# Recurrent scan: 64x64 blocks turned by a transposition instead of by a product with the unit matrix, where the result lies in partitions 0 to 63

## The reference

```python
def rwkv7_step(S, inp):
    r, w, k, v, kk, kka = inp
    sa = jnp.einsum('dbhij,dbhj->dbhi', S, -kk)
    S = S * w[..., None, :] + sa[..., :, None] * kka[..., None, :] + v[..., :, None] * k[..., None, :]
    y = jnp.einsum('dbhij,dbhj->dbhi', S, r)
    return S, y
...
    S0 = jnp.zeros((N_DIR, B, RWKV_HEADS, HEAD_DIM, HEAD_DIM), jnp.float32)
    _, ys = lax.scan(rwkv7_step, S0, xs)
```

## Time and profile before

| | |
|---|---|
| median of three runs | 3591.16 us (3590.39 to 3597.05) |
| profiled execution, its own time | 3590.71 us |
| its span in the profile | 3588.8 us |
| TensorE matmul busy | 3439.0 us, 96% |
| TensorE weight load busy | 2840.0 us, 79% |
| VectorE busy | 1939.6 us, 54% |
| ScalarE busy | 1275.6 us, 36% |
| mean granted TensorE clock | 0.987 of full |

### The profile page before, as it was taken

How to read it: one execution, slowest core, us unless ns; L and a number is a source line. 1 busy time by engine, 2 the same in 40 slices (tenths; PEclk the granted TensorE clock), 3 DMA queues, 4 the chain that set the end, 5 groups by cost and what they waited for, 6 DMA issues and landing times.

```text
span 3588.8 us, 54631 instructions
## 1 busy us (share of the span) xinstructions
PE 3439.0 (96%) x22725; PEld 2840.0 (79%) x22725; DVE 1939.6 (54%) x2632; ACT 1275.6 (36%) x1637; POOL 13.9 (0%) x20
## 2 busy tenths in 40 slices
PE   9999999999999999999999989999899897999998
PEld 7778888887788877778887768888887885888887
DVE  4566646436574654575344455344677666755434
ACT  3474424324442332453223343222532113643223
POOL 0000000000000000000000000000000000000000
PEclk9999999999999999999999999999999999999999
DMA  4102322221122222113222212222224001122222
GB/s 157 59 1 94 103 96 94 94 94 48 65 90 104 94 92 95 51 59 105 94 94 99 88 51 92 103 94 94 93 104 144 16 5 40 58 82 99 99 95 71
DMA packets 50429, 297.06 MB, mean 83 GB/s; under 512 B 6847, under 2 KB 7871, under 8 KB 17348
## 3 DMA queue, kind: packets, MB, share of 16 engines
q1 hardware_dynamic: 39376, 269.92, 21.9%
q10 hardware_dynamic: 10868, 24.41, 1.9%
HBM read 283.99 MB, written 10.33 MB: 82 GB/s over the span
## 4 chain that ended last, share of the span: by engine, by line
PE 85%; DVE 9%; ACT 4%; issue 2%; ACTq 0%; DVEq 0%
PE PS L353 14%; PE PS L355 14%; PE PS L354 14%; PE PS L478 7%; PE PS L479 7%; PE PS L480 7%; PE PS L1997 2%; PE PS L1998 2%; PE PS L1999 2%; PE PS L2522 1%; PE PS L2525 1%; PE PS L2515 1%; PE PS L3014 1%; PE PS L3016 1%; PE PS L3015 1%
## 5 line engine op out<-in xcount | busy, mean ns | idle before, releaser
L172 DVE TENSOR_TENSOR WL<-W,WH 128x2048 fp32r<-128x2048 f32 x249 | 570.8, 2292 | 685.1 <-ACT WH L162 679.5
L162 ACT ACTIVATE WH<-W 128x2048 fp32r<-128x2048 f32 x249 | 476.3, 1913 | 1058.6 <-PE PS L480 552.8
L353 PE MATMUL PS<-XH,WH 128*128 128x512 f32 x2144 | 837.8, 391 | 4.2 <-issue 4.2
L354 PE MATMUL PS<-XL,WH 128*128 128x512 f32 x2144 | 834.9, 389 | 0.0
L355 PE MATMUL PS<-XH,WL 128*128 128x512 f32 x2144 | 834.9, 389 | 0.0
L353 PEld LDWEIGHTS PS<-XH,WH 128*128 128x128 f32 x2144 | 403.0, 188 | 93.6 <-issue 10.6
L354 PEld LDWEIGHTS PS<-XL,WH 128*128 128x128 f32 x2144 | 403.1, 188 | 84.2 <-issue 1.0
L355 PEld LDWEIGHTS PS<-XH,WL 128*128 128x128 f32 x2144 | 402.9, 188 | 84.2
L752 DVE TENSOR_TENSOR PS<-PS,R 128x512 f32<-128x512 f32 x248 | 171.1, 697 | 445.0 <-PE PS L355 440.6
L478 PE MATMUL PS<-HH,WH 128*128 128x512 f32 (+1 forms) x960 | 374.6, 390 | 1.2
L479 PE MATMUL PS<-HL,WH 128*128 128x512 f32 (+1 forms) x960 | 373.6, 389 | 0.0
(11 more groups left out here) (492 smaller groups left out, 4592.4 us busy)
## 6 DMA issues: line engine op xcount, KB each, us to landing
W<-in_weights SPq DMA_DIRECT2D x254, 1024.0 KB, 4.9
gate_spill<-slots ACTq DMA_DIRECT2D x16, 256.0 KB, 2.0
gates<-gate_spill ACTq DMA_DIRECT2D x2, 2048.0 KB
x_spill<-X ACTq DMA_DIRECT2D x1, 2048.0 KB, 8.7
X<-x_spill ACTq DMA_DIRECT2D x1, 2048.0 KB
out<-X ACTq DMA_DIRECT2D x8, 256.0 KB, 2.1
W<-in_weights SPq DMA_DIRECT2D x2, 512.0 KB, 5.0
X<-in_x ACTq DMA_DIRECT2D x4, 256.0 KB, 7.3
```

The lines of the kernel that those rows point to most:

```text
L162: P.e.activation(K.WH[:, s, :], K.W[:, s, :], ACT.Copy).then_inc(P.sem("hi_ready"), P.adds("hi_ready"))
L172: P.e.tensor_tensor(K.WL[:, s, :], K.W[:, s, :], K.WH[:, s, :].bitcast(F32), ALU.subtract).then_inc(P.sem("weights_split"), P.adds("weight ...
L353: P.e.matmul(out, wh[:, k, c], xh[:, k, r], start=(k == 0), stop=False)
L354: P.e.matmul(out, wh[:, k, c], xl[:, k, r], start=False, stop=False)
```

## The change

In `fill`, where t is the lower half, `P.e.transpose` takes the place of the product. Where t is the upper half the product stays. Operands, destination, the order of the quads, the waits and the signals are the same. The lines behind it move down by three.

```diff
             for half, kind in enumerate(kinds):
                 for d, F, t, q, cols in each(c):
                     out = K.PS[t, 6 + d, 256 * half + 64 * q:256 * half + 64 * q + 64]
-                    last = mm(out, src(c, d, kind[0], F, q), K.ident[F, F], start=True, stop=True)
+                    if t.start == 0:
+                        last = P.e.transpose(out, src(c, d, kind[0], F, q), K.ident[F, F])
+                    else:
+                        last = mm(out, src(c, d, kind[0], F, q), K.ident[F, F], start=True, stop=True)
             last.then_inc(P.sem("rows_done"), P.adds("rows_done"))
```

## The result

The changed kernel takes 3636.31 us (median of four runs, 3634.68 to 3638.1), where the kernel before takes 3590.77 (four runs, 3586.43 to 3597.05): a ratio of 1.0126, 95% interval 1.0111 to 1.0141, so it is 1.3% slower. Forecast were 3633 us and a range of 3608 to 3652.

What follows compares the result with a forecast made beforehand. TensorE was taken to bound the kernel. Full-chunk fills +37.8, meta chunk +4, waits -1.7 and -2, clock +4 made +42 us on a median of 3591.16: about 3633 us, range 3608 to 3652.

Steps and rivals of the forecast that it cites:

- TensorE bounds the scan, so a fill's length is the kernel's: Scan: nearly all the chain is TensorE's, so each nanosecond a fill grows is nearly one of the kernel.
- The removed records gain nothing: Fills: 204 matmul records and 204 weight loads go, but corners keeping both products set the pace; gain 0.
- A change of shape empties the array, 0.197 us from record to record: Fills: alternating transpositions and products drains TensorE at each switch and opens the weight load; +4.7 us per full chunk.
- the term of 37.8: Fills of the eight full chunks: added time from changes of shape, +4.7 us per chunk, +37.8 us.
- Meta chunk, +4 us: Fills of the meta chunk: changes of shape add +3.5 us, taken as +4 for a partly lower clock.
- Waits covered, -1.7 us: After the fill of v: the longer fill covers TensorE's waits for c_p of L2599, -1.7 us.
- Waits for "issue", -2 us: TensorE's two largest "issue" groups, 5.0 us: some two fifths go as the array falls behind its sequencer, -2 us.
- The clock, +4 us with two or three stretches: Eight full chunks: light work in the new fills brings two or three stretches at lower clock, +4; bounds 0 and +27.
- Rival 4: The clock falls after nearly every fill: +56 to +60 us, about 3649 us; chance 0.14.
- The sum: Whole kernel: 37.8 + 4 - 1.7 - 2 + 4 = +42 us, median about 3633 us.

Runs made afterwards that it cites:

- the two grouped kernels: All transpositions of a fill ahead of all products, against the changed kernel: 3604.67 us; the same order with products alone: 3601.65 us.
- the runs of the meta chunk alone: Against the changed kernel, transpositions kept in the meta chunk only, full chunks back to products as before: 3596.56 us, ratio 1.0017.
- the grouped kernel: Against the changed kernel, same transpositions and products, but in each fill all transpositions stand ahead of all products: 3604.67 us, ratio 1.0035.

## Why the prediction was right, point by point

**TensorE bounds the scan, so a fill's length is the kernel's.** Right. The fill parts of the steps went from 105.6 to 142.7 us in all, +37.1, and the scan without the meta chunk grew by 37.8.

**The removed records gain nothing.** Right, and shown by the two grouped kernels: corners count, not records. The 0.058 us taken for the record of a transposition, which no row showed, is 0.056 there.

**A change of shape empties the array, 0.197 us from record to record.** The mechanism is right, and shown from three sides: by taking changes away at the same number of transpositions, by halving the transpositions at almost the same number of changes, and by a product of the same shape. The pair of shapes that no row had shown behaves as the three that were. The size was a little high: the round took 0.438 us instead of 0.452. The cause is the transposition's own weight load, 0.105 us long instead of 0.129: a transposition with its load in the open lasts 0.242 us, where I had taken 0.267. That is 3.82 and 2.07 us for the fills instead of 4.0 and 2.2, and 4.48 x 8 = 35.8 us with the lost overlap behind them instead of the term of 37.8.

**Meta chunk, +4 us.** Too low: +7.0 and +5.9 in the two pairs of profiles, +5.8 us by the runs of the meta chunk alone. The clock was in the profile of before, at 0.51 in one part; I allowed half a microsecond for it, and it was at 1.2 GHz through both fills.

**Waits covered, -1.7 us.** This step failed. The wait for c_p stands at the fifth and last `below` of a step, 4 us behind the fill of v (L2442's last record starts at 2943.9 us, the wait is at 2948.1). Its row in the order of time of the kernel before:

```profile
2948.14 0.68 PE L2515 MATMUL PS<-c_p,c_n 64*64 64x64 f32 x16 [0.26 <-DVE c_p L2599]
```

Its 1.7 us are 2.1 in the changed kernel, and 2.1 in the kernel before profiled again. I had read the line and not looked where in the chunk it stands.

**Waits for "issue", -2 us.** They went from 8.2 and 5.9 us to 5.8 and 4.5, but this was no gain, so this step failed too. The two groups of the earlier trace rows, 5.0 us, all stand between `late_sums` and the second `doubled` (4.1 us in the second profile, 1.7 and 1.2 in the changed kernel), where they cost nothing: whether TensorE pauses there for "issue" or waits for c_y, VectorE's mask, the stretch is as long. The same step (that of chunk 1) in the kernel before, then in the changed one:

```profile
2827.52 1.09 PE L2461 MATMUL PS<-ar 64*64 64x128 f32 x32
...
2829.24 1.03 PE L2515 MATMUL PS<-c_p,c_n 64*64 64x64 f32 x29 [0.51 <-issue]
2830.49 0.68 PE L2522 MATMUL PS<-c_y,c_p 64*64 64x64 f32 x16 [0.21 <-DVE c_y L2590]
```

```profile
2845.15 1.09 PE L2464 MATMUL PS<-ar 64*64 64x128 f32 x31
2846.08 1.10 PE L2518 MATMUL PS<-c_p,c_n 64*64 64x64 f32 x32
2848.11 0.68 PE L2525 MATMUL PS<-c_y,c_p 64*64 64x64 f32 x16 [0.94 <-DVE c_y L2593]
```

It is 2.97 us from the first row to the last before, with 0.51 of "issue" and 0.21 of c_y in them, and 2.96 in the changed kernel, with 0.94 of c_y. The wait for c_y went from 2.8 and 3.3 us to 7.2 in both profiles, but the eight stretches from the last product of `late_sums` (L2504 or L2507) to the second `doubled` take 25.7 us in both kernels, and 25.3 and 25.2 in the second pair. So the longer wait is no cost of the change. Less "issue" ahead of this place would have gained next to nothing, which the prediction does not say: here VectorE, not TensorE, sets the time. Why TensorE pauses for "issue" less there stays open. What the longer fills did take away is 1.2 us (0.7 in the second profile) by which the fill parts of the kernel before exceed 8 x 13.05, in pauses that have no row among the waits.

**The clock, +4 us with two or three stretches.** There are two in the first profile (at 2822.4 and 2948.7 us) and one in the second. Each makes its fill part 1.21 us longer (18.74 instead of 17.53), close to the 1.3 worked out from the earlier trace rows: 2.4 and 1.2 us instead of 4. Rival 4 did not come about.

**The sum**, 42 us, against 45.5 (40 to 51 by the interval) and +44.9 in the scan of the first pair of profiles. Set right by what was measured, the terms are 35.8 for the fills, 7.0 for the meta chunk, nothing for the wait for c_p, nothing for "issue", -1.2 for the small pauses in the fill parts and 2.4 for the clock, 44.0 together. The rest of the scan is 1.0 us more ahead of `late_sums`, of which 0.9 lies in chunk 0, whose clock is at 1.2 GHz there, and 0.2 less in the last step. That the forecast came within 3.5 us is in part luck: terms that were too high (2 us for the fills, 1.6 for the clock) stand against terms that were too low (3 for the meta chunk, 2.5 for the waits and pauses, -1.2 instead of -3.7).

No version beats the kernel before: the nearest with transpositions in full chunks, all of them grouped, is 0.35% slower.

## What to carry to other kernels

Small blocks on the corners of the array are cheap as long as all instructions in a row ask for the same shape of rows by columns. An instruction that is shorter by itself but of another shape costs the emptying of the array and an open weight load twice, here 0.13 us net for each change, against 0.03 us for a 64x64 product among others. Before replacing part of a mixed group, look which corner is the busiest one: if the replaced work is not on it, there is nothing to win even at no cost. Where shapes must mix, group them. And a wait that has grown is a cost only if the stretch in which it stands has grown too.

## What the runs showed that I had not expected

- A product of 64 rows by 128 columns between 64x64 products costs as much as the transposition does and more: 4.94 us for the fill of b and k against 3.41 with transpositions in the same order.
- The transposition's weight load of a 64x64 block is shorter than the product's, 0.105 us against 0.129, both in the open.
- With transpositions and products alternating in the fills of the meta chunk the clock stays at 1.2 GHz for 20 us, through the first 9 us of chunk 0 too, also where chunk 0 has no other code than before; with all transpositions of a fill grouped it is 14 us. That is part of why these 24 blocks, a seventeenth of all, cost 6 to 7 of the 45 us.
- A product whose corner is free starts ahead of products that stand before it in the list: in the grouped kernel the first L2520 starts at 2816.20 us, and the last six of L2447, on the two busy corners, from 2816.25 us on.
